# Low-rank products and head sums in split rounded fp32 instead of native fp32, with the 32-row rest stacked three times

## What is computed

```python
Pm = P + (shift_right(P, 1) - P) * mu
r, k, v, xw, xa, xg = split(Pm)                    # 512, 512, 512, 64, 64, 160 columns
w = -softplus(-(w0 + tanh(xw) @ w_up)) - 0.5       # low-rank: 64 -> 512
a = sigmoid(a0 + xa @ a_up)                        # low-rank: 64 -> 512
g = sigmoid(xg) @ g_up                             # low-rank: 160 -> 512
kk = k * k_k
kk = kk / max(norm(kk over a head of 64), 1e-12)   # sum over a head, then a root
k = k * (1 + (a - 1) * k_a)
...                                                # delta-rule state over the positions
bonus = sum(r * k * r_k over a head) * v           # sum over a head
```

## Time and profile before

| | us |
|---|---|
| runs, median of 3 (lowest to highest) | 1009.02 (1008.28 to 1010.4) |
| profiled execution, span | 1007.0 |
| TensorE busy | 978.5 (97%) |
| ScalarE, VectorE, GpSimd busy | 414.1, 404.7, 350.6 |

### The profile page before, as it was taken

How to read it: one execution, slowest core, us unless ns; L and a number is a source line. 1 busy time by engine, 2 the same in 40 slices (tenths; PEclk the granted TensorE clock), 3 DMA queues, 4 the chain that set the end, 5 groups by cost and what they waited for, 6 DMA issues and landing times.

```text
span 1007.0 us, 16980 instructions
## 1 busy us (share of the span) xinstructions
PE 978.5 (97%) x7383; PEld 810.0 (80%) x7383; DVE 404.7 (40%) x634; ACT 414.1 (41%) x622; POOL 350.6 (35%) x151
## 2 busy tenths in 40 slices
PE   6999999989999999999989999999999999999986
PEld 4885878777889998888868888888888888888865
DVE  5110268647645562346424444344344310100445
ACT  5344455336552323253245443444444422322546
POOL 2341443432210000234432434444444344444260
PEclk9999999999999999999989999999999999999999
DMA  8432343321210000123431332333333333233222
GB/s 262 113 86 53 93 104 85 84 85 43 64 43 24 5 4 3 44 83 115 164 98 43 105 104 85 103 100 90 105 92 97 105 106 103 89 99 125 70 78 84
DMA packets 115071, 86.55 MB, mean 86 GB/s; under 512 B 2820, under 2 KB 99990, under 8 KB 114998
## 3 DMA queue, kind: packets, MB, share of 16 engines
q1 hardware_dynamic: 114808, 85.40, 28.7%
q10 hardware_dynamic: 190, 0.08, 0.0%
HBM read 83.37 MB, written 2.10 MB: 85 GB/s over the span
## 4 chain that ended last, share of the span: by engine, by line
PE 74%; ACT 2%; DVE 1%; POOL 1%; issue 1%; POOLq 0%; DVEq 0%; ACTq 0%
PE bank L469 13%; PE bank L471 12%; PE bank L470 12%; PE bank L683 8%; PE bank L513 8%; PE bank L515 8%; PE bank L514 8%; PE bank L702 1%; PE bank L647 1%; PE bank L662 1%; PE bank L635 1%; DVE RX L1583 1%; POOL pleg_w_lo L449 1%; POOLq L194 0%; ACT L944 0%
## 5 line engine op out<-in xcount | busy, mean ns | idle before, releaser
L449 POOL TENSOR_TENSOR w_lo<-raw,w_hi 128x1024 fp32r<-128x1024 f32 x138 | 332.6, 2410 | 624.3 <-ACT w_hi L954 624.3
L954 ACT ACTIVATE w_hi<-raw 128x1024 fp32r<-128x1024 f32 x138 | 146.4, 1061 | 356.1 <-issue 200.8
L469 PE MATMUL bank<-hT_hi,w_hi 128*128 128x512 f32 (+1 forms) x736 | 287.9, 391 | 1.0 <-POOL w_lo L449 0.9
L471 PE MATMUL bank<-hT_hi,w_lo 128*128 128x512 f32 (+1 forms) x736 | 283.3, 385 | 0.0
L470 PE MATMUL bank<-hT_lo,w_hi 128*128 128x512 f32 (+1 forms) x736 | 283.1, 385 | 0.0
L469 PEld LDWEIGHTS bank<-hT_hi,w_hi 128*128 128x128 f32 x736 | 138.3, 188 | 30.4 <-issue 2.1
L471 PEld LDWEIGHTS bank<-hT_hi,w_lo 128*128 128x128 f32 x736 | 138.3, 188 | 27.7
L470 PEld LDWEIGHTS bank<-hT_lo,w_hi 128*128 128x128 f32 x736 | 138.4, 188 | 27.3 <-issue 0.7
L1732 DVE SCALAR_TENSOR_TENSOR cbuf<-bank,params,cbuf 128x511 f32<-128x511 f32 x48 | 36.0, 750 | 133.7 <-ACT cbuf L1273 133.7
L513 PE MATMUL bank<-w_hi,g_hi 128*128 128x512 f32 x184 | 71.7, 389 | 0.0
L515 PE MATMUL bank<-w_hi,g_lo 128*128 128x512 f32 x184 | 71.6, 389 | 0.0
(11 more groups left out here) (264 smaller groups left out, 1311.8 us busy)
## 6 DMA issues: line engine op xcount, KB each, us to landing
raw<-in_w_up_dram SPq DMA_DIRECT2D x48, 512.0 KB, 3.9
raw<-in_w_in_dram SPq DMA_DIRECT2D x33, 512.0 KB, 4.1
raw<-in_w_down_dram SPq DMA_DIRECT2D x24, 512.0 KB, 3.9
raw<-in_w_gate_dram SPq DMA_DIRECT2D x16, 512.0 KB, 3.9
raw<-in_w_out_dram SPq DMA_DIRECT2D x8, 512.0 KB, 3.9
raw<-in_w_ple_gate_dram SPq DMA_DIRECT2D x8, 512.0 KB, 4.0
xs<-in_x_dram SPq DMA_DIRECT2D x4, 512.0 KB, 5.1
raw<-in_w_branch_a_dram SPq DMA_DIRECT2D x4, 512.0 KB, 3.6
```

Of the source, the lines that this page charges most:

```text
L449: nc.gpsimd.tensor_tensor(low(n)[:, :], raw[:, n % RAW_SLOTS, :], high(n)[:, :].bitcast(F32), ALU.subtract).then_inc(*step("pool", ("lo", n)))
L469: nc.tensor.matmul(o, wh, ah, start=first, stop=False)
L471: return nc.tensor.matmul(o, wl, ah, start=False, stop=last)
L954: nc.scalar.activation(high(u)[:, :], raw[:, u % RAW_SLOTS, :], ACT.Copy) \
```

## The change

The low-rank operands and the two addends of the head sums are split into a rounded high part and a rounded low part, and multiplied as rounded fp32: three products for the low-rank ones (high by high, high by low, low by high), two for the sums, whose other factor is exact. For the 32-row rest of g, the weights are loaded three times, into rows 0 to 31, 32 to 63 and 64 to 95; the high and low parts are placed so that one product of 96 rows gives all three terms. lw and la alternate, each in its half of the rows.

ScalarE makes the high parts: those of the low-rank operands and of `heads` directly behind the sigmoids, ahead of rw 3's step; those of the sums behind `squares` (kn) and behind `decays` (bn), and for bn 3 among the v0 units. GpSimd makes the low part of two weight tiles ahead of the low part of unit rw 5. VectorE makes the other low parts: behind shift 3 for the low-rank ones; for the sums in `pre_*`'s order. TensorE waits for all of them. The diff, without the list of semaphore names:

```diff
@@ -255,6 +255,12 @@
 
         lora_x = at("lora_x", 112, [P, 3, SEQ])
         lora_w = at("lora_w", 118, [P, 3, RW])
+
+        lx_hi, lx_lo = [at(n, kb, [P, 2, SEQ], F32R) for n, kb in (("lx_hi", 56), ("lx_lo", 60))]
+        lw_hi, lw_lo = [at(n, kb, [P, 2, RW], F32R) for n, kb in (("lw_hi", 64), ("lw_lo", 68))]
+        lx_3, lw_3 = at("lx_3", 72, [P, SEQ], F32R), at("lw_3", 74, [P, RW], F32R)
+        sum_hi, sum_lo = [at(n, kb, [P, 2, SEQ], F32R) for n, kb in (("sum_hi", 101), ("sum_lo", 105))]
+        heads_r = at("heads_r", 109, [P, P], F32R)
         Lt, Et, Ei, Sc = [at(n, 112 + 4 * i, [P, 2, SEQ]) for i, n in enumerate(("Lt", "Et", "Ei", "Sc"))]
 
         ya_hi = at("ya_hi", 64, [P, NPAIR, SEQ], F32R)
@@ -418,7 +424,8 @@
                     sp.dma_start(lora_w[0:64, 0, :], ins["rw_w_up"][0]).then_inc(lora_in, 16)
                     sp.dma_start(lora_w[64:128, 0, :], ins["rw_a_up"][0]).then_inc(lora_in, 16)
                     sp.dma_start(lora_w[:, 1, :], ins["rw_g_up"][0, 0:P, :]).then_inc(lora_in, 16)
-                    sp.dma_start(lora_w[0:32, 2, :], ins["rw_g_up"][0, P:, :]).then_inc(lora_in, 16)
+                    for r in (0, 32, 64):
+                        sp.dma_start(lora_w[r:r + 32, 2, :], ins["rw_g_up"][0, P:, :]).then_inc(lora_in, 16)
                     sp.dma_start(consts[:, P:], ins["consts"][:, P:]).then_inc(cst_in, 16)
                     sp.dma_start(dist[:, :], ins["dist"]).then_inc(dist_in, 16)
                 if label == ("out", 0, 1):
@@ -445,6 +452,10 @@
             nc.gpsimd.memset(stat[:, epsc + 1:epsc + 2], LN_EPS).then_inc(*step("pool", ("eps",)))
 
             for n in range(len(UNITS)):
+                if n == UIDX[("rw", 5)]:
+                    gp.wait_ge(*done("act", "lora_hi"))
+                    nc.gpsimd.tensor_tensor(lw_lo[:, :, :], lora_w[:, 0:2, :], lw_hi[:, :, :].bitcast(F32), ALU.subtract) \
+                        .then_inc(*step("pool", ("lora_lo",)))
                 gp.wait_ge(*done("act", "hi", n))
                 nc.gpsimd.tensor_tensor(low(n)[:, :], raw[:, n % RAW_SLOTS, :],
                     high(n)[:, :].bitcast(F32), ALU.subtract).then_inc(*step("pool", ("lo", n)))
@@ -570,35 +581,38 @@
                 feature_unit(("rw", i), "rw", i)
 
             pe.wait_ge(cst_in, 16)
-            pe.wait_ge(lora_in, 64)
-            pe.wait_ge(*done("act", "lora_act"))
+            pe.wait_ge(*done("act", "lora_hi"))
+            pe.wait_ge(*done("dve", "lora_lo"))
+            pe.wait_ge(*done("pool", "lora_lo"))
             for i in range(NPAIR):
                 c = slice(i * P, (i + 1) * P)
-                o = begin("lw", i)
-                nc.tensor.matmul(o[:, :], lora_w[0:64, 0, c], lora_x[0:64, 0, :], start=True, stop=True) \
-                    .then_inc(*step("pe", ("lw", i)))
-                o = begin("la", i)
-                nc.tensor.matmul(o[:, :], lora_w[64:128, 0, c], lora_x[64:128, 0, :], start=True, stop=True) \
-                    .then_inc(*step("pe", ("la", i)))
+                ow, oa = begin("lw", i), begin("la", i)
+                for k, (w, x) in enumerate(((lw_hi, lx_hi), (lw_hi, lx_lo), (lw_lo, lx_hi))):
+                    mm = nc.tensor.matmul(ow[:, :], w[0:64, 0, c], x[0:64, 0, :], start=k == 0, stop=k == 2)
+                    if k == 2:
+                        mm.then_inc(*step("pe", ("lw", i)))
+                    mm = nc.tensor.matmul(oa[:, :], w[64:128, 0, c], x[64:128, 0, :], start=k == 0, stop=k == 2)
+                mm.then_inc(*step("pe", ("la", i)))
                 o = begin("lg", i)
-                nc.tensor.matmul(o[:, :], lora_w[:, 1, c], lora_x[:, 1, :], start=True, stop=False)
-                nc.tensor.matmul(o[:, :], lora_w[0:32, 2, c], lora_x[0:32, 2, :], start=False, stop=True) \
+                split3(o[:, :], lw_hi[:, 1, c], lw_lo[:, 1, c], lx_hi[:, 1, :], lx_lo[:, 1, :], True, False)
+                nc.tensor.matmul(o[:, :], lw_3[0:96, c], lx_3[0:96, :], start=False, stop=True) \
                     .then_inc(*step("pe", ("lg", i)))
             for i in range(8, 12):
                 feature_unit(("rw", i), "rw", i)
 
-            def head_sums(tag, src, p):
-
+            def head_sums(tag, p):
+                pe.wait_ge(*done("act", "sum_hi", tag, p))
                 o = begin(tag, p)
-                nc.tensor.matmul(o[:, :], cst("heads"), src, start=True, stop=True).then_inc(*step("pe", (tag, p)))
+                nc.tensor.matmul(o[:, :], heads_r[:, :], sum_hi[:, p % 2, :], start=True, stop=False)
+                pe.wait_ge(*done("dve", "sum_lo", tag, p))
+                nc.tensor.matmul(o[:, :], heads_r[:, :], sum_lo[:, p % 2, :], start=False, stop=True) \
+                    .then_inc(*step("pe", (tag, p)))
 
             def key_norm(p):
-                pe.wait_ge(*done("act", "kk_sq", p))
-                head_sums("kn", Sc[:, p % 2, :], p)
+                head_sums("kn", p)
 
             def bonus_sum(p):
-                pe.wait_ge(*done("dve", "rk", p))
-                head_sums("bn", Sc[:, p % 2, :], p)
+                head_sums("bn", p)
 
             parts = [0]
 
@@ -1020,7 +1034,16 @@
             act.wait_ge(*done("dve", "shift", 14))
             nc.scalar.activation(lora_x[0:64, 0, :], lora_x[0:64, 0, :], ACT.Tanh).then_inc(*step("act"))
             nc.scalar.activation(lora_x[:, 1, :], lora_x[:, 1, :], ACT.Sigmoid).then_inc(*step("act"))
-            nc.scalar.activation(lora_x[0:32, 2, :], lora_x[0:32, 2, :], ACT.Sigmoid).then_inc(*step("act", ("lora_act",)))
+            nc.scalar.activation(lora_x[0:32, 2, :], lora_x[0:32, 2, :], ACT.Sigmoid).then_inc(*step("act"))
+            act.wait_ge(*previous("act"))
+            nc.scalar.activation(lx_hi[:, :, :], lora_x[:, 0:2, :], ACT.Copy).then_inc(*step("act"))
+            for r in (0, 64):
+                nc.scalar.activation(lx_3[r:r + 32, :], lora_x[0:32, 2, :], ACT.Copy).then_inc(*step("act", ("lx_hi", r)))
+            act.wait_ge(lora_in, 16 * 6)
+            nc.scalar.activation(lw_hi[:, :, :], lora_w[:, 0:2, :], ACT.Copy).then_inc(*step("act"))
+            nc.scalar.activation(lw_3[0:96, :], lora_w[0:96, 2, :], ACT.Copy).then_inc(*step("act", ("lora_hi",)))
+            act.wait_ge(cst_in, 16)
+            nc.scalar.activation(heads_r[:, :], cst("heads"), ACT.Copy).then_inc(*step("act"))
             for i in (3, 4, 5, 6, 7):
                 shift_own(i)
             act.wait_ge(*done("dve", "params_rest"))
@@ -1038,9 +1061,20 @@
             for i in range(8, 12):
                 shift_own(i)
 
+            def summed_hi(tag, p):
+                if tag == "kn":
+                    act.wait_ge(*previous("act"))
+                    if p >= 2:
+                        act.wait_ge(*done("pe", "bn", p - 2))
+                else:
+                    act.wait_ge(*done("dve", "rk", p))
+                    act.wait_ge(*done("pe", "kn", p))
+                nc.scalar.activation(sum_hi[:, p % 2, :], Sc[:, p % 2, :], ACT.Copy).then_inc(*step("act", ("sum_hi", tag, p)))
+
             def squares(p):
                 act.wait_ge(*done("dve", "kkr", p))
                 nc.scalar.activation(Sc[:, p % 2, :], KK[:, p, :], ACT.Square).then_inc(*step("act", ("kk_sq", p)))
+                summed_hi("kn", p)
 
             def decays(p):
 
@@ -1061,6 +1095,8 @@
                     squares(i // 3)
                 if i % 3 == 1:
                     decays(i // 3)
+                    if i // 3:
+                        summed_hi("bn", i // 3 - 1)
                 if i % 3 == 2:
                     p = i // 3
                     act.wait_ge(*done("pe", "kn", p))
@@ -1075,6 +1111,8 @@
 
             for s in range(4):
                 before(("v0", s))
+                if s == 1:
+                    summed_hi("bn", NPAIR - 1)
             values("vt0", 0, 512)
 
             def expo(it):
@@ -1426,8 +1464,22 @@
             dve.wait_ge(*previous("dve"))
             c = PARAM_COL["rw_k_a"]
             V.tensor_scalar(stat[:, omka:omka + 4], params[:, c:c + 4], -1.0, 1.0, ALU.mult, ALU.add).then_inc(*step("dve"))
-            for i in (13, 14, 0, 1, 2, 3, 4, 5, 6, 7, 8, 9, 10, 11):
+            for i in (13, 14, 0, 1, 2, 3):
                 shift(i)
+            dve.wait_ge(*done("act", "lx_hi", 64))
+            V.tensor_tensor(lx_lo[:, :, :], lora_x[:, 0:2, :], lx_hi[:, :, :].bitcast(F32), ALU.subtract).then_inc(*step("dve"))
+            V.tensor_tensor(lx_3[32:64, :], lora_x[0:32, 2, :], lx_3[0:32, :].bitcast(F32), ALU.subtract) \
+                .then_inc(*step("dve"))
+            dve.wait_ge(*done("act", "lora_hi"))
+            V.tensor_tensor(lw_3[64:96, :], lora_w[64:96, 2, :], lw_3[64:96, :].bitcast(F32), ALU.subtract) \
+                .then_inc(*step("dve", ("lora_lo",)))
+            for i in (4, 5, 6, 7, 8, 9, 10, 11):
+                shift(i)
+
+            def summed_lo(tag, p):
+                dve.wait_ge(*done("act", "sum_hi", tag, p))
```

(16 more changed lines are left out.)

## The result

The changed kernel takes 1051.7 us (1051.3 to 1052.5), against 1009.1 us of before: a ratio of 1.0425, 95% interval 1.041 to 1.044, or 42.7 us more.

The account below looks back on a forecast made before the run. TensorE's instruction stream plus its holes was taken as the bound. Terms -4.9 + 4.1 - 0.8 + 35.1 + 10.0 = +43.5 us took the span from 1007.0 to 1050.5, with 2.0 around it 1052.5 us; 8-in-10 range 1040 to 1060.

Parts of the forecast that it names:

- stall at rw 5: TensorE waits for rw 5's low part behind new roundings on ScalarE and a GpSimd subtraction: 4.1 us, possibly 5.3.
- gap 1: TensorE's wait at the first kn/bn pair (p = 1), until pre_b and the new subtraction end: 10.1 us.
- gap 2: Wait at pair p = 2, counted from E, the end of qk 6, through pre_c and pre_b: 12.5 us.
- gap 3: Wait at pair p = 3, claimed to repeat gap 2: 12.5 us.
- The new wait: Head sums: TensorE sits in bn p-1 while VectorE goes through pre_b(p), for p = 1, 2, 3: 35.1 us.
- The collision with GpSimd: In pre_c, VectorE meets GpSimd on the shared port; without it gaps 2 and 3 are each 2.2 us shorter.
- Rival D: VectorE and GpSimd collide more or less often: 2.2 us per collision, 1048 to 1057 us; forecast with this spread 0.75.
- The overlap of the two halves of the rows: Low-rank block: rounded 64-row products share slots, as native ones do; otherwise 12 more slots cost 2.7 us.
- rival C: Rounded products of 64 rows or the 96-row one don't run at 0.227 us: 1057 us; chance 0.07.
- The clock: Half clock behind each of four new TensorE holes, 2.5 us each: 10.0 us, ends 0 and 12.8.
- rival A: Long holes, but no lower clock or one that falls under the chain: 1042.5 us; chance 0.12.
- Rival B: The three head-sum waits aren't there, as bn p-1's low part comes in time: 1005 to 1007.5 us; chance 0.06.

Follow-up runs that it names:

- e1: Changed kernel with VectorE making the low part of bn p-1 ahead of pre_b(p) instead of behind it: 1017.8 us.
- e6: Changed kernel with 44 products that nobody reads put ahead of each of bn 0, bn 1 and bn 2: 1046.5 us.
- e5: Changed kernel with low-rank roundings spread, bn's high part ahead of the exponentials, and VectorE's low parts of the sums earlier: 1007.4 us.
- e8: e5 with the exponentials of pairs 2 and 3 behind the root of kn instead of ahead of it: 1003.3 us.
- e7: Changed kernel with only GpSimd's subtraction of the low-rank weights moved two units later: 1049.0 us.
- e3: Only the low-rank part of the change, head sums left in native fp32 as in the kernel before: 1012.2 us.

## Why the prediction was right, step by step

| term | predicted, us | measured, us |
|---|---|---|
| low-rank block | -4.9 | 8.1 - 12.86 = -4.8 |
| stall at rw 5 | +4.1 | +4.2 |
| kn 0 and bn 3 | -0.8 | -0.8 (two parts of 0.4) |
| gap 1 | +10.1 | 158.71 - 146.66 - 1.72 = +10.3 |
| gap 2 | +12.5 | 190.87 - 176.80 - 1.72 = +12.35 |
| gap 3 | +12.5 | 223.97 - 209.90 - 1.72 = +12.35 |
| half clock | +10.0 | 2.6 + 1.8 + 2.7 + 1.6 = +8.7 |
| sum | +43.5 | +42.3 |

The ends of the gaps are the start of L608 and 0.43 us, a product at half clock; 209.90 is 199.02 + 10.88. The half clock is each next unit's length less 5.44: rw 5 from 64.77 to 72.84, qk 6 from 158.71 to 165.92, qk 9 from 190.87 to 199.02, v0 from 223.97 to 231.00.

- **The new wait** was the step that decided, and e1 shows it: the place of one line is worth 34 us. It could be read from the diff alone, and priced from the earlier trace rows: pre_b took 7.16 us in the hole (150.39 to 157.55), 7.15 in the forecast.
- **The collision with GpSimd** in pre_c came, though at another instruction than in the earlier trace rows: the copy of 8 columns at 173.09 took 2.37 us. Where exactly it falls did not matter, once per pre_c did. Rival D's range was wider than needed.
- **The overlap of the two halves of the rows**, which no row of before showed for rounded products, holds; rival C falls.
- **The clock** was the worst-priced term, 1.3 us too high, and that it came so near is in part luck. That half clock follows the long holes is shown, and rival A falls: filling the holes gained 5.3 us (e6). But the 2.5 us a hole were the middle of two rows that do not bear it. The 1.8 us of the transposes were at a granted clock of 1.00, and in the changed kernel the second 14 took 3.25 us, also at 1.00 and after 0.54 us of idle, so that row is no price of a lowered clock. The 3.2 us of the spell at 513 left out what TensorE waits there anyway: from the product at 512.34 (555.87 in the changed kernel, 43.53 us later) to GpSimd's first w_lo behind these weights (534.87 and 577.09, 42.22 us later) the spell cost 1.3 us. The four measured spells, in units where TensorE did not wait for weights, cost 1.6 to 2.7. The Trainium skill, "TensorE: Matmul & The Clock Gate", Part 1, puts the warm-up at under 1% of a typical span; the trace agrees (8.7 of 1049.6 us), but that is a fifth of the change.
- **Rival B** was decided where it was said to be: at VectorE's order. With the order changed and the roundings spread it takes 1007.4 us (e5), at the edge of this rival's range, and with the exponentials moved as well 1003.3 (e8), below it.
- **The rest.** The profiled spans differ by 42.6 us, 0.3 more than the sum. The slower transposes (3.25 us from 11.63 on, where 1.75 is in the earlier trace rows) go with a late start: TensorE wants rw 5 at 60.61, before at 59.56, 1.05 us later. With the sum that is 43.35, and the first copy of the v0 results does come 248.52 - 205.17 = 43.35 us later. The spell at 513, absent in the trace after, takes 1.3 us back. Neither belongs to the change as far as the traces tell: e1's has 1.75 us for the same transposes, e5's a spell from 513 on.
- **Small slips of the sum.** The forecast's own figures give 12.86 - 7.88 = 5.0 us for the low-rank block, not 4.9, and E + 16.85 for pre_b(2), not 16.95; without them it is 43.2.

## What to carry to other kernels

Where an operand of a TensorE-bound kernel is split in two, ask on which queues the parts are made and what stands ahead of them: the products were some 8 us cheaper (4.8 for the block, 0.8 and three times 0.8 for the sums; 6.5 us came through in e8), and one subtraction placed behind a step that itself waits for TensorE cost 34. Follow the cycle by hand, from the product, over the engine that reads it, to the next product in TensorE's order; it needs no run. A hole costs its length and, here behind every one of 4 us and more but the wait for the first load, a spell of half clock, so price both; where the next stretch waits for weights anyway, the spell costs less than its clock says (1.3 us instead of 3.2 at 513).

## What the runs showed of the hardware

- A hole of 2.84 us was followed by half clock once and once not, in the same execution (e6), and once more in e7; the one of 2.25 us ahead of the output projection's weights was before, and was not in the changed kernel. In the four long ones the clock fell 2.5, 4.1, 3.0 and 0.6 us after the last product had ended, and came back 5.3, 4.0, 5.9 and 3.6 us after the restart.
- Useless products in a hole can pay: 132 of them, 5.3 us.
- Which of VectorE and GpSimd gets the shared port went with 0.2 us, and cost TensorE 1 us (e3 against the changed kernel). VectorE's 8-column copy waited 2.2 us for it.
- One product of 96 rows takes the slot of a full one (0.23 us) and needs no change of shape; the pairs of 64 rows need one on either side, 0.2 us each.
